# Left halves of x turned first and two weight pieces multiplied between the turns, in a two-layer decoder trunk

## What is computed

```
for l in range(2):
    xn = rms_norm(x, norm_mix[l])
    h  = xn @ w_in[l]                      # 512 x 1024 times 1024 x 6568
    ... three attention branches from h (dilated with a relative bias, forgetting, latent) ...
    x  = x + (sum of sigmoid(gates) * branch projections) @ w_out[l]
    x  = x + hierarchical_moe(rms_norm(x, norm_ffn[l]), ...)   # 16 SwiGLU experts, top 2 of one group
```

## Time and profile before

| | us |
|---|---|
| median of 3 runs | 1525.13 |
| lowest, highest | 1524.46, 1525.75 |
| profiled execution, span from first to last instruction | 1522.6 |
| TensorE busy in it | 1468.6 (96%) |
| VectorE, ScalarE, GpSimd busy | 925.8, 860.9, 397.5 |
| mean granted TensorE clock | 0.988 of full |

### The profile page before, as it was taken

How to read it: one execution, slowest core, us unless ns; L and a number is a source line. 1 busy time by engine, 2 the same in 40 slices (tenths; PEclk the granted TensorE clock), 3 DMA queues, 4 the chain that set the end, 5 groups by cost and what they waited for, 6 DMA issues and landing times.

```text
span 1522.6 us, 22440 instructions
## 1 busy us (share of the span) xinstructions
PE 1468.6 (96%) x7894; PEld 1142.2 (75%) x7894; DVE 925.8 (61%) x1806; ACT 860.9 (57%) x1660; POOL 397.5 (26%) x554
## 2 busy tenths in 40 slices
PE   8999999999999999999899999999999999999994
PEld 6887777677777787777678867776677777877773
DVE  3555655544554447999854566645445544489996
ACT  5446656655453335888644655565554433468883
POOL 3414227520000013453105053195000000225211
PEclk9999999999999999999999999999999999999997
DMA  7722222142232357999876321222422323769996
GB/s 187 137 76 64 63 60 68 55 117 60 67 97 84 115 185 240 351 364 349 292 192 115 80 63 53 67 70 56 106 67 63 111 84 105 246 224 370 370 360 238
DMA packets 155384, 231.06 MB, mean 152 GB/s; under 512 B 20579, under 2 KB 89955, under 8 KB 155268
## 3 DMA queue, kind: packets, MB, share of 16 engines
q1 hardware_dynamic: 143780, 209.62, 45.6%
...
...
## 4 chain that ended last, share of the span: by engine, by line
PE 83%; DVE 8%; ACT 3%; issue 2%; DMA 2%; ACTq 0%; SPq 0%; POOLq 0%; DVEq 0%
PE bank L545 22%; PE bank L547 20%; PE bank L546 20%; PE bank L1673 4%; PE bank L1658 3%; PE bank L1649 3%; PE bank L1651 3%; DVE xT L617 2%; PE bank L648 2%; ACT xT L611 2%; DVE gate_t L2094 1%; PE bank L1705 1%; DMA q_c<-ytok 1%; PE bank L1708 1%; PE bank L1644 1%
## 5 line engine op out<-in xcount | busy, mean ns | idle before, releaser
L545 PE MATMUL bank<-wh,xT 128*128 128x512 f32 (+1 forms) x960 | 399.3, 416 | 6.5 <-DVE gate_t L2094 4.7
L547 PE MATMUL bank<-wh,xT 128*128 128x512 f32 (+1 forms) x960 | 374.1, 390 | 0.0
L546 PE MATMUL bank<-wl,xT 128*128 128x512 f32 (+1 forms) x960 | 373.3, 389 | 0.0
L486 ACT ACTIVATE wh<-raw,gcol 128x512 fp32r<-128x512 f32 (+1 forms) x208 | 149.0, 717 | 204.6 <-PE bank L547 204.6
L493 DVE SCALAR_TENSOR_TENSOR wl<-raw,gcol,wh 128x512 fp32r<-128x512 f32 (+1 forms) x208 | 161.4, 777 | 135.5 <-ACT wh L486 128.5
L545 PEld LDWEIGHTS bank<-wh,xT 128*128 128x128 f32 x960 | 180.8, 188 | 73.3 <-issue 23.0
L547 PEld LDWEIGHTS bank<-wh,xT 128*128 128x128 f32 x960 | 180.4, 188 | 37.5
L546 PEld LDWEIGHTS bank<-wl,xT 128*128 128x128 f32 x960 | 181.3, 189 | 29.8 <-issue 1.4
L2032 DVE CUSTOM_DVE_ANT_0 prob<-bank,mask 128x128 f32<-128x128 f32 (+3 forms) x128 | 60.5, 490 | 190.0 <-PE bank L1649 100.9
L1820 ACT ACTIVATE prob<-prob,nmax 128x128 f32<-128x128 f32 (+3 forms) x192 | 107.4, 561 | 113.2 <-DVE nmax L2032 112.9
L2336 POOL TENSOR_TENSOR rows<-x_rows,ac 128x512 f32<-128x512 f32 x16 | 22.2, 1404 | 502.8 <-DVE x_rows L2103 502.8
...
## 6 DMA issues: line engine op xcount, KB each, us to landing
...
```

The lines of the kernel that those rows point to most:

```text
L486: nc.scalar.activation(wh[:, i % HL, 0:width], raw[:, i % RAW, 0:width], ACT.Copy, scale=piece_gain(i))\
L545: nc.tensor.matmul(out, lhs[0], rhs[0], start=start, stop=False)
L546: nc.tensor.matmul(out, lhs[0], rhs[1], start=False, stop=False)
L547: return nc.tensor.matmul(out, lhs[1], rhs[0], start=False, stop=stop)
```

## The change

TensorE in both layers now turns left halves of all tiles first, and puts products of pieces 0 and 1 between them: left 0, left 1, piece 0 on tile 0, left 2, piece 0 on tile 1, left 3, then piece 1 on tiles 0 and 1, pieces 0 and 1 on tile 2, and the same on tile 3; then the four right halves; then the loop goes on with piece 2. The semaphores count the halves in the new order, left ones first, and banks 2 and 3 hold the left halves of tiles 2 and 3, banks 4 to 7 the others. ScalarE and VectorE split the right halves at their s == 1, ahead of the squares and of piece 3. In layer 1 VectorE makes the remainder of each left half in the tail of layer 0's experts: add 0, add 1, remainders 0 and 1, add 2, remainder 2, add 3, remainder 3. The bias table moves from s == 2 to s == 3 on TensorE and its copy from s == 3 to s == 4 on ScalarE. Pieces 2 and 3 of layer 0 are issued by ScalarE's queue behind x, not by SyncE's after tile 1. GpSimd waits for tile 1 before it issues the gains, and `sel` comes after them.

```diff
@@ -99,6 +99,9 @@
 OUT1 = START[GID["out", 1]]
 X_BACK = {END[GID["branch", 3]] + RAW + 2 * n: n for n in range(NT)}
 LEFT_TURN = {(OUT1 + 3, 0): 0, (OUT1 + 3, 2): 1, (OUT1 + 4, 0): 2, (OUT1 + 4, 2): 3}
+
+TILE_HALVES = [(n, h) for h in range(2) for n in range(NT)]
+TILE_BANK = {(0, 0): 4, (1, 0): 6, (2, 0): 2, (3, 0): 3, (0, 1): 5, (1, 1): 7, (2, 1): 4, (3, 1): 6}
 
 MERGED_TURN = {OUT0 - 2: range(0, KD // 2), OUT0 + 2: range(KD // 2, KD)}
 
@@ -440,6 +443,28 @@
+        def load_raw(eng, i):
...
+            eng.dma_start(dst, src).then_inc(RAW_SEMS[i % RAW], 16)
@@ -508,7 +533,11 @@
 
         def turn_bank(n, h):
 
-            return bank[(4, 6, 2, 4)[n] + h]
+            return bank[TILE_BANK[n, h]]
+
+        def half_no(n, h):
+
+            return TILE_HALVES.index((n, h)) + 1
 
         def turned_rows(n, h, part):
 
@@ -516,13 +545,13 @@
 
         def turn_hi_of(n, h):
 
-            nc.scalar.wait_ge(wide_done, of(wide_done, 2 * n + h + 1))
+            nc.scalar.wait_ge(wide_done, of(wide_done, half_no(n, h)))
             nc.scalar.activation(turned_rows(n, h, 0), turn_bank(n, h)[:].rearrange("p (k s) -> p k s", k=4), ACT.Copy)\
                 .then_inc(wide_hi, 1)
 
         def turn_lo_of(n, h):
 
-            nc.vector.wait_ge(wide_hi, of(wide_hi, 2 * n + h + 1))
+            nc.vector.wait_ge(wide_hi, of(wide_hi, half_no(n, h)))
             nc.vector.tensor_tensor(turned_rows(n, h, 1), turn_bank(n, h)[:].rearrange("p (k s) -> p k s", k=4),
                                     turned_rows(n, h, 0).bitcast(F32), ALU.subtract).then_inc(wide_lo, 1)
 
@@ -1064,9 +1093,11 @@
             overflow_dve(dve)
             for n in range(NT):
                 add_last(n)
-                if layer + 1 < DEPTH and n == NT - 2:
+                if layer + 1 < DEPTH and n:
                     now[0] = layer + 1
-                    turn_lo_of(0, 0)
+                    if n == 1:
+                        turn_lo_of(0, 0)
+                    turn_lo_of(n, 0)
                     now[0] = layer
 
         def ytok_block(k, n):
@@ -1406,34 +1437,13 @@
             def load_piece(i):
                 if i >= RAW or now[0]:
                     sp.wait_ge(lo_ready, of(lo_ready, max(0, i - RAW + 1)))
...
-                sp.dma_start(dst, src).then_inc(RAW_SEMS[i % RAW], 16)
+                load_raw(sp, i)
 
             def load_bias(q):
                 sp.dma_start(bias_a[16 * q:16 * (q + 1), :, :], skew(bias_dram, q)).then_inc(bias_in, 16)
 
             load_gcol(0)
             for i in range(LEAD):
-                load_piece(i)
-            sp.wait_ge(last_in[1], 16)
-            for i in range(LEAD, RAW):
                 load_piece(i)
             sp.wait_ge(last_in[NT - 1], 16)
             sp.wait_ge(set_ready, 1)
@@ -1514,7 +1524,7 @@
             def bias_table():
 
                 pe.wait_ge(table_in, 32)
-                pe.wait_ge(wide_lo, 4)
+                pe.wait_ge(wide_lo, 2 * NT)
                 for c in range(2):
                     half = BIAS_LEN // 2
                     pe.matmul(bank[6 + c][0:H, 0:half], relb[:], hot[:, c * half:(c + 1) * half],
@@ -1558,19 +1568,33 @@
                 if layer:
                     pe.wait_ge(y_out[1], of(y_out[1], 0))
                 keep_warm(acc[0], 14)
+                def half(n_t, h):
+                    if h == 0 and layer:
+                        pe.wait_ge(x_done, of(x_done, n_t + 1) - NT)
+                    elif h == 0:
+                        pe.wait_ge(last_in[n_t], 16)
+                    if h and n_t >= 2:
+                        pe.wait_ge(wide_lo, of(wide_lo, half_no(n_t - 2, 0)))
+                    for k in range(4):
+                        kt = 4 * h + k
+                        mm = pe.transpose(turn_bank(n_t, h)[:, k * P:(k + 1) * P],
+                                          x_rows[:, n_t, kt * P:(kt + 1) * P], ident[:])
+                    mm.then_inc(wide_done, 1)
+
+                half(0, 0)
+                half(1, 0)
+                piece(0, (0,))
+                half(2, 0)
+                piece(0, (1,))
+                half(3, 0)
+                piece(1, (0,))
+                piece(1, (1,))
+                piece(0, (2,))
+                piece(1, (2,))
+                piece(0, (3,))
+                piece(1, (3,))
                 for n_t in range(NT):
-                    if layer:
-                        pe.wait_ge(x_done, of(x_done, n_t + 1) - NT)
-                    else:
-                        pe.wait_ge(last_in[n_t], 16)
-                    for h in range(2):
-                        if n_t == NT - 1:
-                            pe.wait_ge(wide_lo, of(wide_lo, h + 1))
-                        for k in range(4):
-                            kt = 4 * h + k
-                            mm = pe.transpose(turn_bank(n_t, h)[:, k * P:(k + 1) * P],
-                                              x_rows[:, n_t, kt * P:(kt + 1) * P], ident[:])
-                        mm.then_inc(wide_done, 1)
+                    half(n_t, 1)
 
             def wide_turn(kts):
 
@@ -1592,10 +1616,10 @@
 
                 g, k = PIECES[s]
                 name, idx, nk, width = GROUPS[g]
-                if toks[0] == 0 or s >= NP_ - HL:
+                if toks[0] == 0 or s < LEAD or s >= NP_ - HL:
                     pe.wait_ge(lo_ready, of(lo_ready, s + 1))
                 if g == 0:
-                    pe.wait_ge(wide_lo, of(wide_lo, 2 * toks[-1] + k // 4 + 1))
+                    pe.wait_ge(wide_lo, of(wide_lo, half_no(toks[-1], k // 4)))
                 if s == OUT0 + KD // 2:
                     pe.wait_ge(wide_lo, of(wide_lo, 2 * KD))
                 if k == 0 and toks[0] == 0:
@@ -1713,7 +1737,7 @@
                 now[0] = layer
                 tiles_turn(layer)
                 for s in range(NP_ - HL):
-                    if s == 2 and layer == 0:
+                    if s == 3 and layer == 0:
                         bias_table()
                     if s in MERGED_TURN:
                         wide_turn(MERGED_TURN[s])
@@ -1724,7 +1748,8 @@
                         attend(s, n)
                         if (s, n) in LEFT_TURN:
                             left_right_turn(0, LEFT_TURN[s, n])
-                        piece(s, (n,))
+                        if s >= LEAD:
+                            piece(s, (n,))
                     for key in keys[2:]:
                         other_turn(key)
                 last = range(NP_ - HL, NP_)
@@ -1790,6 +1815,9 @@
             act.dma_start(ident[:], t["ident"]).then_inc(ident_in, 16)
             for n in range(NT):
                 act.dma_start(x_rows[:, n, :], t["x"].rearrange("b (n p) d -> (b n) p d", p=P)[n]).then_inc(last_in[n], 16)
+            now[0] = 0
+            for i in range(LEAD, RAW):
+                load_raw(act, i)
 
             def bias_rows():
 
@@ -1892,13 +1920,15 @@
                     act.wait_ge(y_done, of(y_done, 0))
                 for n in range(NT):
                     turn_hi_of(n, 0)
-                    turn_hi_of(n, 1)
                     if layer == 0 and n < LEAD:
                         split_hi(n, width_of(n))
                 for s in range(NP_):
+                    if s == 1:
+                        for n in range(NT):
+                            turn_hi_of(n, 1)
                     if 1 <= s <= NT:
                         square_rows(0, s - 1, layer)
-                    if s == 3 and layer == 0:
+                    if s == 4 and layer == 0:
                         bias_rows()
                     if s == 6 and layer == 0:
                         rope_tables()
@@ -2136,12 +2166,14 @@
             for layer in range(DEPTH):
                 now[0] = layer
                 for n in range(NT):
-                    if layer == 0 or n:
+                    if layer == 0:
                         turn_lo_of(n, 0)
-                    turn_lo_of(n, 1)
                     if layer == 0 and n < LEAD:
                         split_lo(n, width_of(n))
                 for s in range(NP_):
+                    if s == 1:
+                        for n in range(NT):
+                            turn_lo_of(n, 1)
                     if s == 4 and layer == 0:
                         rope_angles()
                     if s == OUT0:
@@ -2234,12 +2266,13 @@
         def _(pool):
             bounds.extend((pool.to_reg(SEQ - 1), pool.to_reg(3 * SEQ - 1)))
             nc.gpsimd.memset(pw[:], -0.5).then_inc(pool_c, 1)
-            pool.dma_start(sel[:].rearrange("p h q -> p (h q)"), t["sel"]).then_inc(sel_in, 16)
             pool.wait_ge(pool_c, 1)
 
             pool.wait_ge(set_ready, 2)
+            pool.wait_ge(last_in[1], 16)
             for q in range(N_GAINS):
                 load_gain(pool, 0, q)
+            pool.dma_start(sel[:].rearrange("p h q -> p (h q)"), t["sel"]).then_inc(sel_in, 16)
             for layer in range(DEPTH):
                 now[0] = layer
 
```

36 lines of the change are left out of this document (18 added, 18 removed).

## The result

| | before | after |
|---|---|---|
| median, us | 1524.8 | 1534.68 |
| lowest, highest | 1523.94, 1525.75 | 1534.50, 1538.31 |
| span of the profiled execution | 1522.6 | 1532.6 |
| first layer-1 add of expert outputs starts | 760.78 | 765.90 |
| first product of piece 3 in layer 1 | 777.69 | 787.16 |

The changed kernel is slower by a factor of 1.0067, 95% interval 1.0053 to 1.0081: 9.9 us of the medians, 10.0 us of the spans. The two middle marks cut the 10.0 us into parts. Layer 0, up to the first add, is 5.1 us later (the forecast had it 2.4 earlier). From there to piece 3 of layer 1 another 4.35 us go (forecast 5.5), and 0.5 us behind it. So the sign of the forecast held, by layer 1's part; the time of 1528.2 us and the range up to 1531 did not, and what has to be explained is layer 0.

A forecast was written before the change was run, and what follows sets the result against it. The prediction took TensorE, with 83% of the chain, as the bound, so the start of its unbroken run mattered. Layer 0's -2.4 and layer 1's +5.5 us made +3.1: 1525.13 + 3.1 = 1528.2 us, range 1522.5 to 1531.

The forecast's parts named there:

- The start of layer 0: Layer 0, from x's arrival to piece 3: x lands earlier, piece 3 starts at 21.5 against 25.82, gaining 4.3 us.
- Nothing starts early: Rival, layer 0: product (0,0) waits past 14 us for operands; sum 1530; chance 0.23 shared with the slow layer 0 clock.
- Slow clock in layer 0: Rival: clock falls near 11 us, layer 0 gives 0.8 instead of 2.4; 1529.8; chance 0.23 shared with nothing early.
- Piece 8: Layer 0: queued behind the later bias copy, it lands at 35.4 and multiplies at 37.0, cutting the gain to 2.4 us.
- 1.55 us of splits: Layer 0: time added for splits between piece 8's landing at 35.4 and its first product at 37.0.
- Pieces 9 on load in the old rhythm: Layer 0 after piece 8: later weight pieces load as before, so the 2.4 us gain stays.
- Layer 1: VectorE's adds wait behind remainders: last add 3.3 us later, loss 3.9 at full clock, 5.5 with half clock.
- The sum: Whole kernel: layer 0's -2.4 and layer 1's +5.5 make +3.1 us, so slower, 1528.2 us.

The follow-up runs named there:

- layer0_only: The kernel before with the new order and the moved loads in layer 0 alone, layer 1 as before: 1531.19 us, ratio 1.0043.
- after_actcopy: The changed kernel with the copy of the bias rows to DRAM issued by ScalarE on its own queue: 1527.21 us, one execution.
- before_bias_late: The kernel before with only the bias table and its rows moved one piece later: 1531.94 us, ratio 1.0046.
- before_newloads: The kernel before with only the loads moved as in the change: 1523.82 us, ratio 1.0000.
- after_wide: The changed kernel with bias table reads replaced by reads of as many bytes of `w_out` into 128 partitions, bias left out: 1529.44 us, ratio 1.0027.
- after_other: The changed kernel with bias table reads taken from `w_out` into the same 16 partitions each, bias left out: 1539.57 us, one execution.
- l0_actcopy_l1_lag: The changed kernel with ScalarE issuing the bias copy and layer 1's remainders 0 and 1 each one add later: 1521.89 us, ratio 0.9989.
- layer1_only: The kernel before with the new order in layer 1 alone, layer 0 and all loads as before: 1528.85 us, ratio 1.0029.
- after_early: The changed kernel with bias table before the right halves, its rows before their copies, the DRAM copy ahead of piece 7: 1527.87 us, ratio 1.0030.
- after_spread: The changed kernel with the eight bias table reads ahead of pieces 12, 13, 15, 16, 18, 19, 21, 22: 1530.57 us, ratio 1.0035.
- after_lag: The changed kernel with VectorE's layer 1 tail as add 0, add 1, remainder 0, add 2, remainder 1, add 3, remainders 2, 3: 1530.63 us, ratio 1.0048.
- before_actcopy: The kernel before with only the copy of the bias rows issued on ScalarE's queue: 1523.17 us, ratio 0.9996.
- l0_actcopy_l1_old: The new order in layer 0 alone, bias copy issued on ScalarE's queue, layer 1 as in the kernel before: 1522.10 us, ratio 0.9986.

## Why the prediction was wrong, point by point

**The start of layer 0: right.** First product 8.86 (forecast 9.0), last left half turned at 11.78 (forecast 11.0 to 11.5), right halves from 16.35 (15.6), piece 3 at 22.10 (21.5), copy issued at 25.66 (26.4). The moved gain loads cost nothing: the last is issued at 19.86 and `sel` at 20.74, and their first reader stands ahead of piece 9's split, at about 35. The clock was full from about 11 on; the second and third product start 0.43 us apart (9.45, 9.88), at half clock, the later ones 0.23. "Nothing starts early" fell here. "Slow clock in layer 0" did not come true in this profile, but it did in that of layer0_only, where the half clock lasted to about 14.5 and piece 3 came 2.3 us later.

**Piece 8: right mechanism, two terms off.** It landed at 34.63 instead of 35.4. But 1.55 us of splits behind the landing were 3.12. VectorE's queue in after:

```profile
35.41 1.56 DVE L518 SCALAR_TENSOR_TENSOR wl<-raw,gcol,wh 128x512 fp32r<-128x512 f32 x2 [5.97 <-ACT wh L511]
36.88 2.72 DVE L2102 TENSOR_SCALAR rows<-bank,rsx 128x512 f32<-128x512 f32 x4
```

Held up by piece 8, VectorE then splits 8 and 9 in a row and only then empties bank 0 of the sums of pieces 0 to 7 (L2102), which piece 8 needs. TensorE starts 0.9 us into that line. So the gain at piece 8 was 1.65 us, not 2.4.

**"Pieces 9 on load in the old rhythm": the step that failed.** The forecast followed the late copy to the one piece behind it and stopped there; no rival and no bound let layer 0 come out slower than before. What it left out was in the trace of before: DMA engines at a share of 1.08 while the bias table is read back, and landings that rise from 3.2 to 8.0 us over eight reads. From the first read to the landing of the last (33.43 to 61.15) are 27.7 us, so a read and a piece took 3.46 us where TensorE asks for one piece in 2.72. The stream falls back by 0.74 us a pair, 5.9 us in all, against a limit of some 10.9. Started from the 6.0 us of piece 11 in after, instead of 3.2, the same pace ends at 11.9, just past it. after_actcopy shows what that costs: it went from 5.9 to 11.7 us with a stop of 0.47. In after the pace was worse, 4.14 us a pair by the landings of pieces 12 to 18; from 6.8 us at piece 12 that passes the limit with the third pair. With it came the stop of 5.32 us and 1.9 us of half clock. So the late copy explains that the slack was gone, and the pace, whose cause is open, how long the stop was.

before_bias_late shows the late copy alone to be enough, before_newloads that an early TensorE also draws on the same slack, after_wide and after_other that the reads into 16 partitions are what makes the stream slow, and after_actcopy that with pieces 8 and 9 ahead of the copy the stream can be just fast enough; the profile of l0_actcopy_l1_lag, with the same order of issue and a stop of 2.38 us, shows how little is left.

The page "SBUF — State Buffer" of the Trainium skill (section "Door 1: The DMA port swizzle (why `[64,N]` ≈ `[32,N]`)") says that a transfer's rate goes by the ports that its partitions reach, and gives 104 GB/s for partitions 0 to 15 and 328 for 128, each for 1 MiB. An estimate from these figures is 2.5 us for a read of 256 KB and 0.8 for a piece, 3.3 a pair. The 3.46 of before agrees, the 4.14 of after does not. Had the prediction weighed this page, it would have seen that the stream is slower than TensorE there; the rows of before say it too.

**Layer 1: right, a little large.** Forecast: last add 3.3 us later, loss 5.5, bounds 3.9 and 7. Measured: 3.0 us later, loss 4.35 to piece 3, which waited for VectorE's split as said. Behind the last add the forecast had 2.2 us of loss, and 1.36 were measured: the four right-half copies took 2.07 us in a row instead of 2.5, and piece 3 began 5.2 us behind the first right half's turn (781.97) instead of 5.9. The clock was 0.50 for 762 to 764 and for 776 to 778, and full from about 779, 2.3 us behind the first of the 18 products (776.71); forecast 2.5. In the kernels with the new tail the loss from the first add to the end of the span was 3.2, 5.8, 5.8, 4.8 and 5.3 us (layer1_only, after_wide, after_actcopy, after_early, after_spread). With the old tail or the lagged one it was between -1.4 and +1.4. So 5.5 is inside what one profile can tell from 4.35. Of the clock the rows say more than the prediction had: in layer1_only it was full for 762 to 764, with nothing but transposes in that stretch and nothing but 14 transposes in the 9 us ahead of it, and it fell in spite of the products that followed with waits between them. By the rule of the Trainium skill that the prediction weighed (the page "TensorE: Matmul & The Clock Gate", Part 4: PE-mode transpose), transposes bring no full clock; that stretch disagrees too.

**The sum.** -2.4 became +5.1 and +5.5 became +4.4, with 0.5 behind. Without the failed step the sum would have been about 1528, and the range would have held; after_wide, in which the stop near 60 does not come, took 1529.44. That the sign was right is owed to layer 1: layer 0 was to give 2.4 us and took 5.1.

**What stays open.** Why the DMA engines, full in every case, moved so different rates from 46 to 58 us with the same reads and the same pieces: 117 GB/s in before_bias_late, 118 in after_lag, 128 in after, 135 in layer0_only, 139 in before_newloads, but 165 to 170 in before, before_actcopy, layer1_only, after_actcopy and both versions with ScalarE's copy. Where the reads begin does not sort them: 33.99 and 34.74 in after and before_bias_late, 35.23 in l0_actcopy_l1_old with 165 GB/s, 28.73 in before_newloads with 139. Nor does the rate alone sort the stops, since l0_actcopy_l1_lag had one of 2.38 us at 167. Most of after's stop hangs on this pace, so its length is not explained. The weight of the clock in layer 1's loss is open too.
